# Centring the recurrence's values ahead of the scan instead of its outputs behind it, in a fused encoder layer

## The reference

```python
def step(S, inp):
    r_t, w_t, k_t, v_t, a_t, b_t = inp
    sa = jnp.einsum('zbhvk,zbhk->zbhv', S, a_t)
    S = S * w_t[..., None, :] + sa[..., None] * b_t[..., None, :] + v_t[..., None] * k_t[..., None, :]
    return S, jnp.einsum('zbhvk,zbhk->zbhv', S, r_t)
...
y = ys[0] + jnp.flip(ys[1], axis=1)
mean = jnp.mean(y, axis=-1, keepdims=True)
var = jnp.mean((y - mean) ** 2, axis=-1, keepdims=True)
y = ((y - mean) * lax.rsqrt(var + LNX_EPS)).reshape(B, T, C)
y = y * lnx_g.astype(f32) + lnx_b.astype(f32)
```

## Time and profile before

| | us |
|---|---|
| median of 3 runs | 3146.86 (3140.73 to 3148.6) |
| the profiled execution | 3151.79 |
| its span | 3150.0 |
| PE busy | 2923.0 (93%) |
| DVE busy | 1311.4 (42%) |
| ACT busy | 934.0 (30%) |
| POOL busy | 625.7 (20%) |

### The profile page before, as it was taken

The page is one execution under the profiler, slowest core; times in us unless marked ns, Lnnn a source line. Parts: engine busy times, 40 slices in busy tenths (PEclk is TensorE's granted clock), DMA queues, the critical chain, the costliest instruction groups (busy, mean ns, idle before and its releaser), DMA issues. The chain is left out here.

```text
span 3150.0 us, 44992 instructions
## 1 busy us (share of the span) xinstructions
PE 2923.0 (93%) x18736; PEld 1804.1 (57%) x18736; DVE 1311.4 (42%) x2187; ACT 934.0 (30%) x1576; POOL 625.7 (20%) x370
## 2 busy tenths in 40 slices
PE   4799999999999997999999989966989999999999
PEld 3466666666666664677777777743434444444443
DVE  3374453656555363676675545434321111110110
ACT  3323232332323241566565445532210000000000
POOL 0141322314132131000001042340133233220000
PEclk9899999999999998999999999988989999999999
DMA  2143434424252443135103677626321111103100
GB/s 72 40 156 97 147 114 123 143 74 160 87 167 93 138 144 104 38 76 132 37 26 93 129 176 178 126 79 209 100 74 40 40 54 40 40 27 154 40 27 27
DMA packets 188856, 300.88 MB, mean 96 GB/s; under 512 B 84544, under 2 KB 121184, under 8 KB 182128
## 3 DMA queue, kind: packets, MB, share of 16 engines
q1 hardware_dynamic: 176560, 251.02, 27.8%
q10 hardware_dynamic: 12096, 46.99, 3.7%
HBM read 190.64 MB, written 107.32 MB: 95 GB/s over the span
## 5 line engine op out<-in xcount | busy, mean ns | idle before, releaser
L494 PE MATMUL pp_ps<-uT,pp_w 128*128 128x347 f32 x3072 | 909.2, 457 | 19.5 <-DMA pp_w<-in_w_main 19.5
L494 PEld LDWEIGHTS pp_ps<-uT,pp_w 128*128 128x128 f32 x3072 | 580.4, 190 | 335.4 <-DMA pp_w<-in_w_main 20.2
L1285 DVE TENSOR_REDUCE at_mn<-at_S 128x1 f32<-128x1040 f32 x128 | 156.1, 1239 | 52.8 <-PE at_S L1116 52.8
L1176 PE MATMUL at_ob<-at_v,at_pT 128*128 128x128 f32 (+1 forms) x1152 | 175.2, 292 | 0.0
L1116 PE MATMUL at_S<-at_kR,at_qR 64*128 64x512 f32 (+1 forms) x768 | 163.8, 502 | 9.5 <-ACT at_v L1213 5.1
L2035 PE MATMUL fh_b<-u2T,fh_w 128*128 128x512 f32 x352 | 161.3, 601 | 6.5 <-DMA fh_w<-in_w_ffn_in 6.5
L2175 PE MATMUL fd_ps<-fd_more,hidden 128*128 128x512 f32 x384 | 165.8, 592 | 0.0
L719 POOL TENSOR_TENSOR pp_neighbours<-pp_raw 128x1040 f32<-128x1040 f32 x24 | 47.8, 1993 | 566.9 <-ACT pp_raw L584 369.0
L2035 PE MATMUL fh_b<-u2T,fh_ws 128*128 128x512 f32 x352 | 158.2, 592 | 0.0
L2035 PE MATMUL fh_b<-fh_t,fh_ws 128*128 128x512 f32 x352 | 154.7, 592 | 0.0
L1176 PEld LDWEIGHTS at_ob<-at_v,at_pT 128*128 128x128 f32 (+1 forms) x1152 | 143.5, 191 | 15.4
(11 more groups left out here) (244 smaller groups left out, 4216.8 us busy)
## 6 DMA issues: line engine op xcount, KB each, us to landing
pp_w<-in_w_main SPq DMA_DIRECT2D x64, 512.0 KB, 3.8
s_kept<-pp_ob ACTq DMA_DIRECT2D x48, 520.0 KB, 4.3
fh_w<-in_w_ffn_in SPq DMA_DIRECT2D x44, 512.0 KB, 4.2
rc_kb<-s_kb SPq DMA_DIRECT2D x64, 256.0 KB, 6.7
rc_aw<-s_ar SPq DMA_DIRECT2D x64, 256.0 KB, 7.1
s_ar<-pp_ar SPq DMA_DIRECT2D x8, 1088.0 KB, 4.0
s_kb<-pp_kb SPq DMA_DIRECT2D x8, 1088.0 KB, 6.3
s_vz<-pp_vz SPq DMA_DIRECT2D x8, 1088.0 KB, 7.5
```

The source lines that it names most:

```text
L494: ins = nc.tensor.matmul(ps[s][:, n, 0:NW], weights, moving[:, n * NW:(n + 1) * NW], start=(k == 0), stop=(k == len(parts) - 1))
L1176: ins = nc.tensor.matmul(ob[:, 0:P], pT[t % 2][0:mk, b, 0:P], v[h % 2][0:mk, b, :], start=(b == 0), stop=(b == NBLK - 1))
L1285: nc.vector.tensor_reduce(mn[t % 2][:, m:m + 1], S[m][:, 0:T], AX, ALU.min).then_inc(least[m], 1)
```

## The change

`turn` multiplies the values by `centre` where it transposed them, so that their rows come out turned and centred. Outputs are then centred, and the centring products, their ACT copies and the list `LN` go. POOL squares yT itself as soon as the outputs are there, and finishing reads yT and writes yc. The variance products stand at s = 14, 15 and, for the outer pieces, at s = 2, 3 of the next round.

```diff
-LN = [(what, piece) for pair in ((0, 1), (2, 3)) for what in ("centre", "vary") for piece in pair]
-INNER_AT, OUTER_AT, RAISED_AT = 13, 1, 5
+INNER_DONE, INNER_AT, OUTER_AT, RAISED_AT = 12, 14, 2, 5
...
-            if s >= INNER_AT:
+            if INNER_AT <= s < INNER_AT + 2:
                 return p, s - INNER_AT
-            if p > 0 and OUTER_AT <= s < OUTER_AT + 4:
-                return p - 1, 4 + s - OUTER_AT
+            if p > 0 and OUTER_AT <= s < OUTER_AT + 2:
+                return p - 1, 2 + s - OUTER_AT
...
                 def square(p, n):
                     g, part = PIECES[n]
-                    pool.wait_ge(ln_kept, ln(p, "centre", n))
+                    pool.wait_ge(y_kept, NY * p + (NY if part == "outer" else INNER_DONE))
                     if n >= 2:
-                        pool.wait_ge(ln_made, ln(p, "vary", n - 2))
+                        pool.wait_ge(ln_made, len(PIECES) * p + n - 1)
                     elif p > 0:
-                        pool.wait_ge(ln_made, ln(p - 1, "vary", n + 2))
-                    centred = part_of(yc[:, g, :], part)
-                    nc.gpsimd.tensor_tensor(sq[n % 2][:], centred, centred, ALU.mult).then_inc(squared, 1)
+                        pool.wait_ge(ln_made, len(PIECES) * (p - 1) + n + 3)
+                    y = part_of(yT[p % 2][:, g, :], part)
+                    nc.gpsimd.tensor_tensor(sq[n % 2][:], y, y, ALU.mult).then_inc(squared, 1)
...
-                        ins = nc.tensor.transpose(p_rv[:, g, 2 * P:3 * P], vz[:, g, held(q), :], ident[:])
+                        ins = nc.tensor.matmul(p_rv[:, g, 2 * P:3 * P], vz[:, g, held(q), :], centre[:], start=True, stop=True)
...
                 def normalise(p, n):
-                    what, piece = LN[n]
-                    g, part = PIECES[piece]
                     if p > 0 or n > 0:
-                        pe.wait_ge(ln_kept, len(LN) * p + n)
-                    if what == "centre":
-                        if piece % 2 == 0:
-                            pe.wait_ge(y_kept, NY * p + (NY if part == "outer" else INNER_AT - 1))
-                        nc.tensor.matmul(p_ln[:], centre[:], part_of(yT[p % 2][:, g, :], part), start=True, stop=True).then_inc(ln_made, 1)
-                    else:
-                        pe.wait_ge(squared, len(PIECES) * p + piece + 1)
-                        nc.tensor.matmul(p_ln[:], means[:], sq[piece % 2][:], start=True, stop=True).then_inc(ln_made, 1)
+                        pe.wait_ge(ln_kept, len(PIECES) * p + n)
+                    pe.wait_ge(squared, len(PIECES) * p + n + 1)
+                    nc.tensor.matmul(p_ln[:], means[:], sq[n % 2][:], start=True, stop=True).then_inc(ln_made, 1)
```

More of the change, by code:

```diff
@@ L1354, in normalised_at @@
             p, s = q // NS, q % NS
-            if s >= INNER_AT:
+            if INNER_AT <= s < INNER_AT + 2:
                 return p, s - INNER_AT
-            if p > 0 and OUTER_AT <= s < OUTER_AT + 4:
-                return p - 1, 4 + s - OUTER_AT
-            return None
-        def ln(p, what, piece):
-            return len(LN) * p + LN.index((what, piece)) + 1
+            if p > 0 and OUTER_AT <= s < OUTER_AT + 2:
+                return p - 1, 2 + s - OUTER_AT
+            return None
         def four(ap):
@@ L1451, in finish @@
                     pool.wait_ge(scale_made, done)
-                    nc.gpsimd.tensor_tensor(y, y, part_of(scale[:, g, :], part), ALU.mult).then_inc(scaled, 1)
+                    if n < 2 and p > 0:
+                        pool.wait_ge(mr_stored, 16 * (2 * (p - 1) + 2))
+                    nc.gpsimd.tensor_tensor(y, part_of(yT[p % 2][:, g, :], part), part_of(scale[:, g, :], part),
+                                            ALU.mult).then_inc(scaled, 1)
                     pool.wait_ge(scaled, done)
@@ L1603, in _ @@
                         products(q + 2)
-                for n in range(4, len(LN)):
+                for n in range(2, len(PIECES)):
                     normalise(ROUNDS - 1, n)
@@ L1618, in keep_rows @@
                     ins.then_inc(rv_kept, 1)
[L1620 to L1625, removed]
                 def keep_logs(p, piece):
                     g, part = PIECES[piece]
-                    act.wait_ge(ln_made, ln(p, "vary", piece))
+                    act.wait_ge(ln_made, len(PIECES) * p + piece + 1)
                     if p > 0:
@@ L1636, in raise_logs @@
                     g, part = PIECES[piece]
-                    act.wait_ge(ln_kept, ln(p, "vary", piece))
+                    act.wait_ge(ln_kept, len(PIECES) * p + piece + 1)
                     logs = part_of(scale[:, g, :], part)
                     nc.scalar.activation(logs, logs, ACT.Exp, scale=-0.5).then_inc(scale_made, 1)
-                def keep_ln(p, n):
-                    what, piece = LN[n]
-                    (keep_centred if what == "centre" else keep_logs)(p, piece)
                 act.wait_ge(eps_set, 1)
@@ L1660, in _ @@
                         if s == 1 and p > 1:
-                            act.wait_ge(ln_made, ln(p - 2, "centre", len(PIECES) - 1))
+                            act.wait_ge(mr_done, len(PIECES) * (p - 1))
                         src = p_y[:, 0:4 * CH].rearrange("p (g z t) -> p g z t", g=2, z=2)
@@ L1665, in _ @@
                     if normalised_at(q):
-                        keep_ln(*normalised_at(q))
+                        keep_logs(*normalised_at(q))
                     if p > 0 and s in (RAISED_AT, RAISED_AT + 1):
@@ L1671, in _ @@
                     raise_logs(ROUNDS - 1, piece)
-                for n in range(4, len(LN)):
-                    keep_ln(ROUNDS - 1, n)
+                for piece in range(2, len(PIECES)):
+                    keep_logs(ROUNDS - 1, piece)
                 for piece in range(2, len(PIECES)):
@@ L1728, in finish @@
                     dve.wait_ge(scale_made, done)
-                    nc.vector.scalar_tensor_tensor(y, y, table[:, par("lnx_g", 2 * p + g)], part_of(scale[:, g, :], part),
-                                                   ALU.mult, ALU.mult).then_inc(last_gained, 1)
+                    nc.vector.scalar_tensor_tensor(y, part_of(yT[p % 2][:, g, :], part), table[:, par("lnx_g", 2 * p + g)],
+                                                   part_of(scale[:, g, :], part), ALU.mult, ALU.mult).then_inc(last_gained, 1)
                     dve.wait_ge(last_gained, n - 1)
```

## The result

The changed kernel takes 3161.38 us (median of 5 runs, 3158.51 to 3165.03) where the kernel before takes 3144.52 (median of 5): a ratio of 1.0052, interval 1.0040 to 1.0063. It is slower by 17 us; 3168 had been predicted, 21 us above the kernel before.

The account below looks back on a forecast made before the run. The prediction took PE to bound the kernel, busy for 93% of the span and pacing the recurrence. Its terms, -8.4 + 12.0 + 12.1 + 5.1 = +20.8 us on 3146.9, gave 3168 us, range 3152 to 3182.

Parts of the forecast that it names:

- The turn: Products replace the value transposes in each recurrence step: 0.24 us a step, 50 of 68 turns on the path, +12.0 us.
- rival (c): In the turn, a product takes four times a transpose: 0.66 us a step, +42 us, 3189 us; chance 0.04.
- The centring products: Of 16 products of 1.05 us leaving the recurrence, 8 in or from rounds 0 to 2 pay: -8.4 us.
- The step behind the wait: Rounds 1 to 3: variance products one step earlier wait for POOL's squares, leaving a clean step more behind: +12.1 us.
- The clock: After each of three new PE waits for POOL, a stretch at half clock costs 1.7 us: +5.1 us.
- Rival (b): POOL's squares in rounds 1 to 3 are there in time, no wait or low clock: +1.6 us, 3148 us; chance 0.06.

Follow-up runs that it names:

- e4_transpose_turn: The changed kernel with the turn transposing the values again, so that nothing is centred: 3162.80 us, 1.0046 against the kernel before.
- e8_changed_tail: The changed kernel with POOL's inner squares ahead of its gates and the last round's outer squares ahead of finishing: 3134.34 us, 0.9952 against the kernel before.

## Why the prediction was right, point by point

The sum can be laid beside the two profiles stretch by stretch; a stretch of the forecast is made of its own terms. The forecast of the first stretch has 0.5 us for the two turns ahead of the loop, which the measured one, from the first `make_w`, doesn't; without them it is 2.0 against 2.0.

| stretch | forecast us | measured us |
|---|---|---|
| round 0 and the two first turns | +2.5 | +2.0 |
| round 1 up to step 8 | -0.2 | -2.2 |
| round 1 from step 8 | +7.8 | +6.0 |
| round 2 up to step 8 | -0.2 | +0.3 |
| round 2 from step 8 | +7.4 | +7.0 |
| round 3 up to step 5 | -0.9 | -1.6 |
| round 3 from step 5 to POOL's finishing | +4.5 | +2.9 |
| the end | 0 | 0 |
| sum | +20.9 | +14.4 |

*The turn.* Forecast 0.24 us a step, measured 0.23 in every clean step, with products at twice a transpose; the factor of four that rival (c) needed is contradicted by 0.22 against 0.11 and by the doubled transposes. The runs with the turn alone came to 7 us, not to the 14 that the steps add up to, and this is the term that was mis-sized most. What the forecast lacked is that PE's waits for code change too: in the profiles of the changed kernel they are 5 and 8 us less than in that of the kernel before. These waits are likely most of what separates 17 from 21; but the two series of the same kernel gave 17 and 12, so the size of the miss is not known better than that.

*The centring products.* 8.4 us back, as forecast; the inner ones of rounds 1 to 3 went into the wait for POOL, and the last two changed nothing, since POOL sets the end.

*The step behind the wait.* The waits were forecast at 9.6, 11.2 and 2.9 us and are 9.24, 10.59 and 1.16. That moving the product back takes 13 us off, and moving the squares ahead more, confirms the mechanism; the 12.1 us themselves are not measured apart from the clock's share and the waits for code. In round 1 the gates began 34.4 us after the start of step 8 (1864.05 - 1829.64) instead of 35.8, which took 1.4 us off. The third wait was shorter because PE lost 1.56 us to code in step 7 of that round.

*The clock.* Forecast 1.7 us after each of three waits; measured 1.5 and 2.0 after the two long ones, nothing after the one of 1.16. That was the mis-sized part: 3.5 instead of 5.1.

*Rival (b)*, the squares in time, was priced at +1.6 us; when the order on POOL made it true, it came to -6 (-9 to -3). Its price left out that the wait of 1.96 us that the kernel before had in round 1 goes too, and the waits for code, 16.6 us against 18.7. In the profiles the recurrence is 3.0 us shorter, which these cover; the rest of the 6 is open, as is the surplus of the same order on the kernel before.

What stays open is the code itself. Over all profiles its waits sum to 8.3 to 18.7 us where a step takes 5.33 and to 15.8 to 20.6 where it takes 5.10, with overlap. That PE can run ahead of its code is shown, by the blocks of 256 instructions; why 9 to 14 of some 56 blocks cost a wait and the others none is not, and by how much a given edit changes these waits could not be forecast here.

## What to carry to other kernels

When an edit moves an operation to an earlier place in a queue, ask first what its input waits for in the producer's queue: here the outputs to be squared were complete at 1858.5 us in round 1 and POOL came to them at 1874.2, 16 us later, and the order of two lines on POOL decided between 6 us gained and 17 lost. A product spread over every step (136 of 128 columns) can cost as much as the 16 products of 512 that it replaces; count columns and instructions before calling it free. And idle time that ends with "issue" is a budget of its own, here 8 to 21 us of some 430, in code that is written out without loops: read it in both profiles before a difference of some us is put down to the edit.

## What the runs showed of the hardware that was not expected

PE's float32 product of 128 x 128 by 128 columns shows as two instructions of 0.11 us and is not to be told from two transposes, neither in the step (5.33 and 5.32 us) nor in the time (1.0021 and 1.0020).

PE waits for its own code for 0.2 to 3.9 us at a time, in any of its operations but always at the same place of a block of 256 instructions, as told ahead of the single experiments. In `e4_transpose_turn` such a wait of 2.51 us was followed by 3.4 us at half the clock, and the step took 8.96 instead of 5.10 us with the wait; behind one of 2.59 us in the changed kernel's profile the clock stayed at 1.00.

Rows of POOL and DVE are longer where both work on SBUF at the end of the fastest kernel (`e8_changed_tail`, one profile): POOL's multiplication by a scalar (L1453) takes 2.02 us beside DVE and 1.57 alone, DVE's addition (L1710) 1.06 and 1.63 us where it takes 0.69 alone. Not every row is: DVE's product (L1713) stays at 0.69.
